# State products of a token mixer moved between two halves of a projection, and convolution pieces at a group's boundary moved ahead of them

## The chip, the cores and the metric

The kernel runs on one core of one Trainium2 chip. The metric is the device time of one execution in microseconds (us). The median of three runs before the change is 2328.43 us (2327.97 to 2331.13). The execution that was profiled took 2326.24 us; its trace spans 2324.4 us from the first to the last instruction.

## The reference

One decoder layer over 2048 tokens of width 1024: a hybrid mixer, cross attention over 256 memory tokens, a mixture of experts, a final norm. The change touches the mixer alone, which projects the normed tokens and runs retention and a Mamba-2 state space (SSD) in chunks of 128 tokens:

```python
proj = hn @ w_in
q, k, v, g, z, xbc, dt_raw, u = jnp.split(proj, splits, axis=-1)
# retention, per chunk
s = einsum('bhcid,bhcjd->bhcij', qc, kc) * decay;  y_in = einsum(s, vc)
kv = einsum('bhcjd,bhcje->bhcde', k_dec, vc)          # carried state S of retention
# SSD, per chunk, after a causal convolution of 4 taps and silu on xbc
CB = einsum('bclgn,bcsgn->bcgls', Cc, Bc)
y_diag = einsum(CB * Lmat, xdt)
states = einsum('bclgn,bclgrp->bcgrpn', Bc, xdt * decay_states)
S = S * chunk_decay + states                           # carried state S of the SSD
y_off = einsum('bclgn,bcgrpn->bclgrp', Cc, S_prev) * exp(A_cum)
```

## The kernel before, in words

The mixer handles 16 chunks q of 128 tokens in 4 groups g of 4 chunks. The order of the work on every engine is written out by hand: each engine has its own list of steps, and the engines meet through semaphores that count finished instructions.

At a group's start TensorE (PE) turns the group's normed rows into eight tiles of columns (turn, L849). ScalarE (ACT) writes the near half-precision part of each (take_hn, L502), and VectorE (DVE) writes the rest that is left over (hn_rest, L622). Every projection is then three half-precision products for each of eight tiles, 24 matmuls of 128x512 in a row (products, L111). First the eight pieces of the convolution's input are projected for the whole group (project_conv); the first of them waits until all eight rests are there. ACT copies each out of PSUM (L512), DVE convolves it (L632 to L643).

Then the chunks follow one another. While PE works on chunk q it also projects chunk q+1, in pieces put between the small products of chunk q: dt and u (project_dt), queries and keys (project_qk), value and gate columns (project_vg, two halves of 12 matmuls each), z (project_z). The small products of a chunk, in this order, are:

- turn_qk_x (L910, L914), decays (L922, L924), segments (L931);
- inner: C times B (L937) and queries times keys (L942);
- states: C times the carried SSD state (L949), and B times the decayed inputs (L955). L955 writes the PSUM bank that holds C times B, so it waits until DVE's first mask (L718) has read that bank;
- retained: retention's outputs (L118 with vb and S_r) and its new state (L970);
- results: the SSD's inner outputs (L118 with xdt and E).

The small products share three PSUM banks in turn (room); the projections have four other banks (slot) and one for queries and keys. DVE's list for a chunk is: segment inputs (L703), steps of dt (L672 to L698), xdt (L707), decayed xdt (L712), rotation of the next chunk's queries and keys (rotate, L660 to L666), the masks (weights: L718, L721, L724), in the first chunk of a group also the norm of the next group's rows (L603, L606), states (L730, L733, L736), retained (L743 to L747), results (L752 to L765).

The last chunk of a group is handled at the boundary, among the turns and convolution pieces of the next group, and there are three such boundaries; the 16th chunk is handled alone at the end. In the 12 other chunks the loop over q runs. The lists are in the functions marked vector and tensor; L775 to L787 and L991 to L1000 are the boundaries, L1017 to L1030 PE's loop over chunks.

Of the kernel before, what the change touches and what calls it, by code (L numbers as in the profile page):

```python
# [27 lines left out]
KT = D // P  # L28
# [200 lines left out]
def mixer_projections(nc, env, dram, rooms, begun):  # L229
# [5 lines left out]
    with ExitStack() as ctx:  # L235
# [364 lines left out]
        def _(dve):  # L600
# [19 lines left out]
            def hn_rest(g, kt):  # L620
                dve.wait_ge(taken, g * BIG + kt + 1)
                dve.scalar_tensor_tensor(hn_s[1][:, kt, :], bank[kt % 4][:, :], gmix_s[:, kt:kt + 1], hn_s[0][:, kt, :], ALU.mult, ALU.subtract).then_inc(hn_lo, 1)  # L622
# [77 lines left out]
            def segments(q):  # L700
                dve.wait_ge(dt_ready, q + 1)
                dve.wait_ge(ch_done, q)
                dve.tensor_tensor(segin[:, :, :], bc(le, 1, SH), bc(dtA[:, q % GC, :], 2, P), ALU.mult).then_inc(seg_ready, 1)  # L703

            def steps_in(q):
                dve.wait_ge(s_act, q * N_ACT + 2)
                ch.post(dve.tensor_tensor(xdt[:, :, :], xtok[:, :, :], bc(dt_[:, q % GC, :], 2, SP_), ALU.mult))  # L707
                ch.wait()
# [58 lines left out]
            for g in range(NG):  # L767
                q0 = g * GC
                if g:
                    q = q0 - 1  # L770
                    segments(q)
                    hn_rest(g, 0)
                    hn_rest(g, 1)
                    steps_in(q)
                    hn_rest(g, 2)  # L775
                    hn_rest(g, 3)
                    steps_decayed(q)
                    hn_rest(g, 4)
                    hn_rest(g, 5)
                    weights(q)  # L780
                    hn_rest(g, 6)
                    hn_rest(g, 7)
                    states(q)
                    conv(g, 0)
                    retained(q)
                    conv(g, 1)
                    results(q)  # L787
                else:
                    for kt in range(KT):
                        hn_rest(g, kt)  # L790
                    for i in range(1, N_E):
                        early_rest(i)
                    dve.wait_ge(a_set, 1)
                    dve.wait_ge(k_ld, 32)
                    dve.wait_ge(c_ld, 16 * 11)
                    dve.tensor_scalar(a_bc[:, :], a_bc[:, :], -1.0, None, ALU.mult).then_inc(a_set, 1)
                    dve.wait_ge(a_set, 2)
                    dve.wait_ge(w_lo, N_E)
                    dve.wait_ge(s_set, 5)
                    conv(g, 0)  # L800
                    conv(g, 1)
                for ct in range(2, KT):
                    conv(g, ct)
                dt_bias(q0)
                dt_one(q0)
                dt_rest(q0)
                rotate(q0)
                for q in range(q0, q0 + GC - 1):
                    segments(q)
                    dt_bias(q + 1)  # L810
                    steps_in(q)
                    dt_one(q + 1)
                    steps_decayed(q)
                    dt_rest(q + 1)
                    rotate(q + 1)
                    weights(q)
                    if q == q0 and g < NG - 1:
                        norm(g + 1)
                    states(q)
                    retained(q)  # L820
                    results(q)
            q = NCH - 1
# [12 lines left out]
        def _(pe):  # L835
# [8 lines left out]
            def turn(g, kt):  # L844
                o = slot(g, kt)
                if kt == 0:
                    pe.wait_ge(xs_done, g * GC + GC)
                for c in range(GC):
                    ins = pe.transpose(o[:, c * P:(c + 1) * P], xg[:, c, kt * P:(kt + 1) * P], ident)  # L849
                ins.then_inc(big, 1)  # L850

            def project_conv(g, ct):
                if g == 0 and ct % 2 == 0:
                    pe.wait_ge(w_lo, ct // 2 + 1)
                if ct == 0:
                    pe.wait_ge(taken, g * BIG + KT)
                    pe.wait_ge(hn_lo, g * KT + KT)
                o = slot(g, KT + ct)
                w = [[wi[:, h, kt, C_XBC + ct * P:C_XBC + (ct + 1) * P] for kt in range(KT)] for h in range(2)]
                hn = [[hn_s[h][:, kt, :] for kt in range(KT)] for h in range(2)]  # L860
                products(pe, o[:, :], w, hn).then_inc(big, 1)
# [19 lines left out]
            def project_vg(q, half):  # L881
                g, n = q // GC, 2 * KT + 3 * (q % GC) + 1
                ins = project(q, bank[n % 4] if half else slot(g, n), C_VG, 2 * RW, HALF[half])
                if half:
                    ins.then_inc(big, 1)
# [47 lines left out]
            def inner(q):  # L933
                tok = slice(q % GC * P, (q % GC + 1) * P)
                o = room(q, 5)
                for k in range(2):
                    ins = pe.matmul(o[:, k * P:(k + 1) * P], xc[:, 4 + k, tok], xc[:, 6 + k, tok], start=True, stop=True)  # L937
                ins.then_inc(small, 1)
                pe.wait_ge(s_act, q * N_ACT + 1)
                o = room(q, 6)  # L940
                for h in range(RH):
                    ins = pe.matmul(o[:, h * P:(h + 1) * P], kT[:, h // 2, :], qz[:, h // 2, h % 2, :], start=True, stop=True)  # L942
                ins.then_inc(small, 1)

            def states(q):
                tok = slice(q % GC * P, (q % GC + 1) * P)
                o = room(q, 7)
                for k in range(2):
                    ins = pe.matmul(o[:, k * 256:(k + 1) * 256], xc[:, 6 + k, tok],  # L949
                                    S_m[:, 4 * k:4 * k + 4, :].rearrange("p h e -> p (h e)"), start=True, stop=True)  # L950
                ins.then_inc(small, 1)
                o = room(q, 8)
                pe.wait_ge(s_dve, q * N_DVE + 1)
                for k in range(2):
                    ins = pe.matmul(o[:, k * 256:(k + 1) * 256], btok[:, k, :], xdec[:, k * 256:(k + 1) * 256], start=True, stop=True)  # L955
                ins.then_inc(small, 1)
# [23 lines left out]
            for g in range(NG):  # L980
                q0 = g * GC
                if g:
                    q = q0 - 1
                    turn_qk_x(q)
                    turn(g, 0)
                    turn(g, 1)
                    decays(q)
                    turn(g, 2)
                    turn(g, 3)
                    segments(q)  # L990
                    turn(g, 4)  # L991
                    turn(g, 5)
                    inner(q)
                    turn(g, 6)
                    turn(g, 7)
                    states(q)
                    project_conv(g, 0)
                    retained(q)
                    project_conv(g, 1)
                    results(q)  # L1000
                else:
                    for kt in range(KT):
                        turn(g, kt)
                    project_conv(g, 0)
                    project_conv(g, 1)
                for ct in range(2, KT):
                    project_conv(g, ct)
                if g == 0:
                    pe.wait_ge(w_lo, N_E)
                project_dt(q0)  # L1010
                if g == 0:
                    pe.wait_ge(l_lo, KT)
                for part in (project_qk, project_vg, project_z):
                    part(q0, 0)
                    part(q0, 1)
                for q in range(q0, q0 + GC - 1):
                    turn_qk_x(q)  # L1017
                    project_dt(q + 1)
                    decays(q)
                    segments(q)  # L1020
                    project_qk(q + 1, 0)
                    project_qk(q + 1, 1)
                    inner(q)
                    states(q)
                    project_vg(q + 1, 0)
                    project_vg(q + 1, 1)
                    retained(q)
                    results(q)
                    project_z(q + 1, 0)
                    project_z(q + 1, 1)  # L1030
            q = NCH - 1
# [1849 lines left out]
```

## Time and profile before

| | before |
|---|---|
| median of three runs | 2328.43 us (2327.97 to 2331.13) |
| profiled execution | 2326.24 us |
| its span | 2324.4 us, 43924 instructions |
| PE busy | 2121.5 us (91%) |
| DVE busy | 1449.3 us (62%) |
| ACT busy | 974.8 us (42%) |
| POOL busy | 502.6 us (22%) |
| mean granted TensorE clock | 0.966 |

The mixer is the first 679 us of the span; the S5 mixer, the attention and the experts follow, each behind a barrier of all engines. A row of the timeline gives the start in us from the span's start, how long the row lasted, the engine, line and operation, what it wrote and read, how many instructions it merges, and in brackets how long the engine had been idle before it and who ended that. Consecutive matmuls overlap in the pipeline, so the time that a block holds PE is read from the start of one row to the start of the next, not from a row's length. A float32 matmul stands in the trace as two records.

### The profile page before, as it was taken

The page shows a single profiled execution, that of the slowest core. Times are in us where ns is not written, and L with a number is a line of the kernel's source. Part 1 is how long each engine was busy: PE and PEld are TensorE (multiplying, and loading weights), DVE is VectorE, ACT ScalarE, POOL GpSimd, SP SyncE. Part 2 cuts the span into 40 slices and gives each one's busy share as a digit, 9 for nine tenths or more (in the row PEclk, how much of TensorE's full clock was granted, in tenths as well). Part 3 has the DMA queues.
Part 4 walks back from the last instruction along what each step waited for, and adds up shares of the span by engine and source line. Part 5 has one row for each costly group of instructions (what it writes and reads, how often), then busy time and mean ns, then how long its engine had stood idle before and what let it go on. Part 6 is the DMA issues. An engine that isn't in the chain of part 4 may idle for free. (4 is left out here: it accounts for less than half of the span.)

```text
span 2324.4 us, 43924 instructions
## 1 busy us (share of the span) xinstructions
PE 2121.5 (91%) x15061; PEld 1207.6 (52%) x15062; DVE 1449.3 (62%) x2501; ACT 974.8 (42%) x1470; POOL 502.6 (22%) x378
## 2 busy tenths in 40 slices
PE   7999999999979897999999999659999999999990
PEld 3455554555658873455555555325555555555450
DVE  7566565665668864344445454477566777777763
ACT  5432533333321333222222222147566677667653
POOL 0022121121220000001111011133333443444433
PEclk9999999999989999999999999879999999999995
DMA  8101001011050134112112110089889999999958
GB/s 254 51 28 64 1 28 64 1 28 48 10 227 28 56 127 173 55 37 73 46 64 73 37 46 37 37 305 353 256 277 315 325 342 347 344 336 332 343 167 305
DMA packets 160842, 350.96 MB, mean 151 GB/s; under 512 B 29866, under 2 KB 40490, under 8 KB 160464
## 3 DMA queue, kind: packets, MB, share of 16 engines
q1 hardware_dynamic: 140416, 311.37, 36.8%
q0 software_dynamic: 19152, 33.74, 6.4%
q10 hardware_dynamic: 1152, 4.19, 0.5%
q8 instruction: 80, 1.31, 0.2%
q14 instruction: 42, 0.34, 0.0%
HBM read 299.94 MB, written 58.26 MB: 154 GB/s over the span
## 5 line engine op out<-in xcount | busy, mean ns | idle before, releaser
L2690 PE MATMUL bankE<-wgu,xT 128*64 128x512 f16 x3840 | 429.9, 380 | 20.1 <-issue 11.7
L2690 PEld LDWEIGHTS bankE<-wgu,xT 128*64 128x64 f16 x3840 | 218.3, 110 | 223.1 <-issue 36.7
L2587 DVE SCALAR_TENSOR_TENSOR wgu<-w_rows,wgu 128x2048 f16<-128x2048 f32 x128 | 284.8, 2286 | 37.2 <-ACT wgu L2441 37.1
L111 PE MATMUL bankA<-main_room,hnT 128*128 128x512 f16 (+1 forms) x1536 | 303.2, 355 | 4.1 <-DVE main_room L646 4.1
L2389 POOL DMA_INDIRECT scratch_ybuf<-y,rows x80 | 173.2, 2165 | 376.6 <-DMA scratch_ybuf<-y,rows 276.5
L2441 ACT ACTIVATE wgu<-w_rows 128x2048 f16<-128x2048 f32 x128 | 234.3, 1899 | 34.4 <-issue 27.0
L111 PEld LDWEIGHTS bankA<-main_room,hnT 128*128 128x128 f16 x1536 | 149.9, 98 | 148.5 <-issue 10.3
L2690 PE MATMUL bankE<-wd,hT 128*64 128x512 f16 x1920 | 222.5, 381 | 0.4 <-ACT hT L2472 0.4
L2587 DVE SCALAR_TENSOR_TENSOR wd<-w_rows,wd 128x2048 f16<-128x2048 f32 x64 | 143.8, 2288 | 54.5 <-ACT wd L2441 51.7
L111 PE MATMUL bankA<-hnT,main_room 128*128 128x512 f16 x768 | 169.0, 381 | 8.9 <-issue 6.8
L111 PE MATMUL bankC<-w_out_s,catT 128*128 128x512 f16 x768 | 170.1, 382 | 2.5 <-DVE w_probs L2056 2.5
L111 PE MATMUL vbank<-w_probs,probsT 128*128 128x512 f16 x768 | 171.9, 381 | 0.0
L111 PE MATMUL bankC<-main_room,hnT_c 128*128 128x512 f16 x768 | 170.7, 379 | 0.0
L2690 PEld LDWEIGHTS bankE<-wd,hT 128*64 128x64 f16 x1920 | 102.1, 110 | 96.1 <-issue 13.9
L1887 POOL TENSOR_TENSOR rs_c<-ms_c,nhalf_c 128x1 f32<-128x1 f32 x32 | 17.7, 554 | 557.1 <-DVE ms_c L2016 557.1
L2381 POOL DMA_INDIRECT xr<-scratch_xn_scr,rows x82 | 119.5, 1457 | 78.5 <-PE bankE L2663 46.4
L2441 ACT ACTIVATE wd<-w_rows 128x2048 f16<-128x2048 f32 x64 | 118.9, 1903 | 26.6 <-issue 25.3
L111 PEld LDWEIGHTS bankA<-hnT,main_room 128*128 128x128 f16 x768 | 74.8, 98 | 100.0 <-issue 12.4
L111 PEld LDWEIGHTS bankC<-w_out_s,catT 128*128 128x128 f16 x768 | 75.4, 98 | 91.7 <-DVE w_probs L2056 3.4
L111 PEld LDWEIGHTS bankC<-main_room,hnT_c 128*128 128x128 f16 x768 | 75.2, 98 | 84.1
L111 PEld LDWEIGHTS vbank<-w_probs,probsT 128*128 128x128 f16 x768 | 74.2, 98 | 85.1 <-issue 1.3
L2599 DVE SCALAR_TENSOR_TENSOR sg<-bankE,gate_of,sg 128x256 f32<-128x256 f32 x80 | 38.3, 479 | 92.7 <-ACT sg L2462 92.5
(390 smaller groups left out, 2992.1 us busy)
## 6 DMA issues: line engine op xcount, KB each, us to landing
w_rows<-in_w_gate SPq DMA_DIRECT2D x64, 1024.0 KB, 8.3
w_rows<-in_w_up SPq DMA_DIRECT2D x64, 1024.0 KB, 9.6
w_rows<-in_w_down SPq DMA_DIRECT2D x64, 1024.0 KB, 9.1
cat_t<-scratch_cat SPq DMA_DIRECT2D x16, 512.0 KB, 4.8
main_room<-in_x SPq DMA_DIRECT2D x16, 512.0 KB, 5.6
scratch_ybuf<-main_room SPq DMA_DIRECT2D x16, 512.0 KB, 2.6
out<-hf SPq DMA_DIRECT2D x16, 512.0 KB, 11.1
x_room<-in_x SPq DMA_DIRECT2D x3, 2048.0 KB, 10.9
```

Of the source, the lines that this page charges most:

```text
L111: ins = pe.matmul(o, a[x][k], b[y][k], start=start and k == 0 and j == 0, stop=stop and k == n - 1 and j == 2)
L1887: pool.tensor_tensor(rs[:, k, c:c + 1], ms[:, k, c:c + 1], nhalf[:, 0:1], ALU.pow).then_inc(rsd, 1)
L2381: pool.indirect_dma_start(xr[:, b % 2, :], None, from_rows, bass.IndirectOffsetOnAxis(ap=rows[:, b:b + 1], axis=0), bounds_check=2 * T - 1 ...
L2389: pool.indirect_dma_start(to_rows, bass.IndirectOffsetOnAxis(ap=rows[:, b:b + 1], axis=0), y[b % 2], None, bounds_check=2 * T - 1, oob_is_ ...
L2441: act.activation(place(p, slot, 0), room(p), ACT.Copy, scale=W_SCALE).then_inc(done, 1)
L2587: dve.scalar_tensor_tensor(place(p, slot, 1), room(p), W_SCALE, place(p, slot, 0), ALU.mult, ALU.subtract).then_inc(done, 1)
L2599: dve.scalar_tensor_tensor(sg[:, p, :], GB[p][:, DE // 2:], gate_of[:, bass.ds(b, 1)], sg[:, p, :], ALU.mult, ALU.mult).then_inc(hr, 1)
L2690: ins = pe.matmul(o(half), tokens(x, k), rows(z, k, half), start=k == 0 and j == 0, stop=k == n - 1 and j == 2, skip_group_check=True)
```

## The change

On PE, in the 12 chunks of the loop, the first half of the next chunk's value and gate columns goes ahead of the state products, which then stand between the two halves. At the three boundaries the first convolution piece goes ahead of the state products, and the second ahead of retention's products. On DVE, at the boundaries, the three masks go behind all eight rests (before, two rests stood behind them). Nothing is added or removed. ACT, POOL and the DMA queue on SP keep their order.

```diff
@@ vector, boundary
                     steps_decayed(q)
-                    hn_rest(g, 4)
-                    hn_rest(g, 5)
+                    for kt in range(4, KT):
+                        hn_rest(g, kt)
                     weights(q)
-                    hn_rest(g, 6)
-                    hn_rest(g, 7)
                     states(q)
                     conv(g, 0)
@@ tensor, boundary
                     turn(g, 7)
+                    project_conv(g, 0)
                     states(q)
-                    project_conv(g, 0)
+                    project_conv(g, 1)
                     retained(q)
-                    project_conv(g, 1)
                     results(q)
@@ tensor, loop over chunks
                     inner(q)
+                    project_vg(q + 1, 0)
                     states(q)
-                    project_vg(q + 1, 0)
                     project_vg(q + 1, 1)
                     retained(q)
                     results(q)
```

PE in the loop over chunks, before: state products (L949, L955) right behind the inner products (L937, L942), then the 24 matmuls of the next chunk's value and gate columns (L111), then retention (L118).

```order
L937 MATMUL bankA<-xc 128x128
L942 MATMUL bankA<-qz,PT 128x128 [waits small_taken_act]
L942 MATMUL bankA<-qz,PT 128x128 x3
L949 MATMUL bankA<-S_m,xc 128x256 [waits small_taken_act]
L949 MATMUL bankA<-S_m,xc 128x256
L955 MATMUL bankA<-segin,btok 128x256 [waits small_taken_dve]
L955 MATMUL bankA<-segin,btok 128x256
L111 MATMUL bankA<-main_room,hnT 128x512 [waits big_taken]
L111 MATMUL bankA<-main_room,hnT 128x512 x23
L118 MATMUL bankA<-vb,PT 64x64 [waits small_taken_dve,big_taken]
```

Here L955 is the first instruction behind the inner products that waits for DVE. The same place now; the file is two lines shorter above it, so L935, L940, L947 and L953 are the former L937, L942, L949 and L955.

```order
L935 MATMUL bankA<-xc 128x128
L940 MATMUL bankA<-qz,PT 128x128 [waits small_taken_act]
L940 MATMUL bankA<-qz,PT 128x128 x3
L111 MATMUL bankA<-main_room,hnT 128x512 [waits big_taken]
L111 MATMUL bankA<-main_room,hnT 128x512 x11
L947 MATMUL bankA<-S_m,xc 128x256 [waits small_taken_act]
L947 MATMUL bankA<-S_m,xc 128x256
L953 MATMUL bankA<-segin,btok 128x256 [waits small_taken_dve]
L953 MATMUL bankA<-segin,btok 128x256
L111 MATMUL bankA<-main_room,hnT 128x512 x12
L118 MATMUL bankA<-vb,PT 64x64 [waits small_taken_dve,big_taken]
```

Twelve of the 24 matmuls have moved ahead of the state products; the instruction that waits for DVE's mask (semaphore small_taken_dve) now stands behind them.

PE at a boundary now, from the last turns (L847, formerly L849): the first convolution piece, with its wait for the rests (hn_rest), stands right behind the turns.

```order
L847 MATMUL bankA<-cst_a,x_room 128x128 [waits hn_rest,big_taken]
L847 MATMUL bankA<-cst_a,x_room 128x128 x3
L111 MATMUL bankA<-hnT,main_room 128x512 [waits big_taken,hn_rest]
L111 MATMUL bankA<-hnT,main_room 128x512 x23
L947 MATMUL bankA<-S_m,xc 128x256 [waits small_taken_act]
L947 MATMUL bankA<-S_m,xc 128x256
L953 MATMUL bankA<-segin,btok 128x256 [waits small_taken_dve]
L953 MATMUL bankA<-segin,btok 128x256
L111 MATMUL bankA<-hnT,main_room 128x512 [waits hn_rest,big_taken]
L111 MATMUL bankA<-hnT,main_room 128x512 x23
L118 MATMUL bankA<-vb,PT 64x64 [waits small_taken_dve,big_taken]
```

Before, the two state products stood between the turns and that piece, and the second piece stood behind retention's products.

DVE at a boundary, before: rests (L622) on both sides of the masks (L718, L721, L724).

```order
L712 TENSOR_TENSOR segin<-xdt,dec 128x512 [waits small_taken_act]
L622 SCALAR_TENSOR_TENSOR hnT<-bankA,gmix_s,hnT 128x512 [waits big_taken,dve_steps_a]
L622 SCALAR_TENSOR_TENSOR hnT<-bankA,gmix_s,hnT 128x512 [waits big_taken]
L718 TENSOR_TENSOR PT<-bankA,cst_a 128x256 [waits small_done]
L721 TENSOR_TENSOR E<-E,PT 128x1024 [waits small_taken_dve]
L724 TENSOR_TENSOR PT<-bankA,cst_a 128x512 [waits small_done,dve_steps_a]
L622 SCALAR_TENSOR_TENSOR hnT<-bankA,gmix_s,hnT 128x512 [waits big_taken,small_taken_dve]
L622 SCALAR_TENSOR_TENSOR hnT<-bankA,gmix_s,hnT 128x512 [waits big_taken]
L730 TENSOR_TENSOR segin<-bankA,dec 128x512 [waits small_done]
```

The last two rests, for which the first convolution piece waits, stand behind the masks here. DVE at a boundary now:

```order
L712 TENSOR_TENSOR segin<-xdt,dec 128x512 [waits small_taken_act]
L622 SCALAR_TENSOR_TENSOR hnT<-bankA,gmix_s,hnT 128x512 [waits big_taken,dve_steps_a]
L622 SCALAR_TENSOR_TENSOR hnT<-bankA,gmix_s,hnT 128x512 [waits big_taken] x3
L718 TENSOR_TENSOR PT<-bankA,cst_a 128x256 [waits small_done]
L721 TENSOR_TENSOR E<-E,PT 128x1024 [waits small_taken_dve]
L724 TENSOR_TENSOR PT<-bankA,cst_a 128x512 [waits small_done,dve_steps_a]
L730 TENSOR_TENSOR segin<-bankA,dec 128x512 [waits small_done,small_taken_dve]
```

The masks have moved behind the last two rests, straight ahead of the state step (L730).

## Rows read from the trace of the kernel before

**Rows 1.** Page, busy time, share of the span and instructions of each engine.
```profile
PE 2121.5 (91%) x15061; PEld 1207.6 (52%) x15062; DVE 1449.3 (62%) x2501; ACT 974.8 (42%) x1470; POOL 502.6 (22%) x378
```

**Rows 2.** Waits, 0 to 560 us: total us, times, longest us.
```profile
PEld bankA L955 <- DVE PT L718: 9.5, 12, 0.9
...
PE bankA L111 <- issue: 6.8, 3, 2.3
...
PE bankA L118 <- DVE S_m L736: 0.9, 3, 0.3
```

**Rows 3.** Timeline of PE in one chunk of the loop (columns as told above).
```profile
124.67 5.34 PE L111 MATMUL bankA<-main_room,hnT 128*128 128x512 f16 x24
129.85 0.61 PE L937 MATMUL bankA<-xc 128*128 128x128 f32 x4
130.29 1.06 PE L942 MATMUL bankA<-qz,PT 128*128 128x128 f32 x8
131.19 1.03 PE L949 MATMUL bankA<-S_m,xc 128*128 128x256 f32 x4
132.73 1.10 PE L955 MATMUL bankA<-segin,btok 128*128 128x256 f32 x4 [0.52 <-DVE PT L718]
133.67 5.34 PE L111 MATMUL bankA<-main_room,hnT 128*128 128x512 f16 x24
138.95 0.34 PE L118 MATMUL bankA<-vb,PT 128*64 128x64 f32 x4
...
141.20 5.35 PE L111 MATMUL bankA<-main_room,hnT 128*128 128x512 f16 x24
```

**Rows 4.** Timeline of DVE in the same chunk.
```profile
132.16 0.42 DVE L718 TENSOR_TENSOR PT<-bankA,cst_a 128x256 f32<-128x256 f32 x1
...
134.60 0.69 DVE L730 TENSOR_TENSOR segin<-bankA,dec 128x512 f32<-128x512 f32 x1
...
135.93 0.69 DVE L736 TENSOR_TENSOR S_m<-S_m,bankA 128x512 f32<-128x512 f32 x1
```

**Rows 5.** Timeline of PE in the first chunk of a group.
```profile
112.21 1.15 PE L118 MATMUL bankA<-xdt,E 128*64 128x64 f32 x32 [0.29 <-DVE S_m L736]
```

**Rows 6.** Timeline of DVE in that chunk.
```profile
107.50 2.74 DVE L606 TENSOR_SCALAR x_room<-x_room,rstd_a 128x1024 f32<-128x1024 f32 x4 [1.13 <-POOL rstd_a L414]
...
111.47 0.69 DVE L736 TENSOR_TENSOR S_m<-S_m,bankA 128x512 f32<-128x512 f32 x1
```

**Rows 7.** Timeline of PE at the first boundary, from the last turns.
```profile
182.31 1.04 PE L849 MATMUL bankA<-cst_a,x_room 128*128 128x128 f32 x8
183.19 1.03 PE L949 MATMUL bankA<-S_m,xc 128*128 128x256 f32 x4
184.34 1.10 PE L955 MATMUL bankA<-segin,btok 128*128 128x256 f32 x4
187.72 5.34 PE L111 MATMUL bankA<-hnT,main_room 128*128 128x512 f16 x24 [2.28 <-issue]
...
200.68 14.63 PE L111 MATMUL bankA<-hnT,main_room 128*128 128x512 f16 x67
```

**Rows 8.** Timeline of DVE at that boundary.
```profile
182.45 1.41 DVE L622 SCALAR_TENSOR_TENSOR hnT<-bankA,gmix_s,hnT 128x512 f16<-128x512 f32 x2
183.78 0.41 DVE L718 TENSOR_TENSOR PT<-bankA,cst_a 128x256 f32<-128x256 f32 x1
...
186.21 1.41 DVE L622 SCALAR_TENSOR_TENSOR hnT<-bankA,gmix_s,hnT 128x512 f16<-128x512 f32 x2
...
193.88 0.55 DVE L635 TENSOR_SCALAR xc<-xbcT,cw,cb 128x512 f32<-128x512 f32 x1 [4.27 <-ACT xbcT L512]
```

**Rows 9.** Timeline of ACT at that boundary.
```profile
181.54 2.68 ACT L502 ACTIVATE hnT<-bankA,gmix_s 128x512 f16<-128x512 f32 x4
```

**Rows 10.** Timeline of PE at the third boundary.
```profile
507.62 6.86 PE L111 MATMUL bankA<-hnT,main_room 128*128 128x512 f16 x24 [2.28 <-issue]
```

**Rows 11.** Stretch behind it: length, busy of PE, PEld, DVE, ACT, POOL, granted clock.
```profile
508.00:510.00 2.00, 2.00 (x6) 0.73 (x5) 1.48 (x4) 0.00 (x0) 0.00 (x0) 0.50 0.04 8
```

## The prediction

> **What bounds the kernel now.** I read the busy times first: PE is busy for 91% of the span and every other engine for 62% or less [rows 1], so in the mixer I look for what PE waits for. The waits view of the first 560 us names three kinds at the places that the change touches [rows 2]. The weight load of L955 waits 12 times for DVE's first mask (L718), 9.5 us in all, 0.79 us each. A projection (L111) waits 3 times, 6.8 us in all; the view names no releaser ("issue"). And results (L118) wait 3 times for the carried SSD state (L736), 0.9 us in all. The timelines place them. In a chunk of the loop PE issues L949 at 131.19 us and L955 at 132.73, 0.15 us behind the end of the mask at 132.16 + 0.42 = 132.58 [rows 3, 4]. At a boundary the first convolution piece starts at 187.72, idle for 2.28 us before, 0.10 us behind the end of the last rests (186.21 + 1.41 = 187.62): the unnamed releaser is DVE's L622 [rows 7, 8]. PE has no slack in the loop, since each block starts where the last one ends, so what PE saves there the time saves; the later stages start behind a barrier and are moved as a whole.
>
> **The chunks of the loop.** Nothing is added or removed; twelve matmuls go ahead of four. From L949 to retention the old order takes 138.95 - 131.19 = 7.76 us [rows 3]. The new one, from the same rows: a block of 24 ahead of a float32 product takes 129.85 - 124.67 = 5.18, so the first half 2.59; L955 takes 133.67 - 132.73 = 0.94, and L949, which has the same shape, I put at 0.94 too (it was never seen without the wait behind it); the second half, with the step over to retention, 5.28 - 2.59 = 2.69. The sum is 7.16, which saves 0.60. The split adds two steps between half precision and float32 that no row shows between these very blocks. From below they cost nothing: 5.18 / 24 = 0.216 us a matmul leaves no room for one ahead of L937. From above 0.10 each, the excess of 5.28 over 5.18 ahead of retention. So 0.40 to 0.60 a chunk; I take 0.55, near the row of L937, which is the same kind of step.
>
> Does the wait go? L955 would issue at 131.19 + 2.59 + 0.94 = 134.72, and the mask was read out by 132.58: 2.1 us of cover [rows 3, 4]. What is late next? DVE's state step now follows L949 and L955: it starts at about 134.8 instead of 134.60, and its last part (L736, 0.69 us) waits for the end of L955 near 135.8, so it is over near 137.0 instead of 136.62. Retention starts on PE at 131.19 + 7.16 = 138.35 and results, which need that state, behind it. At least 1.3 us are left. Behind the waiting L730 on DVE stand only the state step and retention's copies, which themselves wait for PE.
>
> In the first chunk of groups 0 to 2 this fails. There DVE puts the norm of the next group's rows (2.74 us, from 107.50) ahead of the state step, which ends at 111.47 + 0.69 = 112.16; results start at 112.21, having waited 0.29 us already [rows 5, 6]. DVE's times there do not depend on the state products, so results still start at 112.21 and what PE saved becomes a longer wait. These 3 chunks give 0 (from below also 0: no instruction of DVE is later). The other 9 of the 12 give 9 x 0.55 = 5.0 us (3.6 to 5.4).
>
> **The three boundaries.** The masks took DVE from 183.78 to 186.21, 2.43 us. Behind all rests now, they let the seventh and eighth rest start at 183.78, if ACT has written those tiles: its four copies end at 181.54 + 2.68 = 184.22, 0.67 each, so the seventh is there at 183.55 and the eighth before 184.45, when DVE comes to it [rows 8, 9]. The rests end at 185.19, and the first convolution piece starts at 185.29, 2.43 us earlier. But the state products stood in that idle time for nothing, and now they are on PE's path with 2 x 0.94 = 1.88 us. Block by block: 185.29 + 5.18 (piece) + 1.88 + 5.28 (second piece up to retention) + 2.25 (retention and results, 141.20 - 138.95 in rows 3) = 199.88 for the third piece, which started at 200.68 [rows 3, 7]. That saves 0.80 a boundary. The lower end leaves the four blocks from 187.72 to 200.68 as long as they were together (12.96): 2.43 - 1.88 = 0.55. The upper end is 0.90, one step of 0.10 less. I take 0.80, since the rows of the loop show the very sequence retention, results, projection: 2.4 us for the three (1.7 to 2.7).
>
> The change adds a wait on DVE: L730 now stands until L949 is over at 185.29 + 5.18 + 0.94 = 191.4, while the masks are done at about 187.5. Queued behind it are the rest of the state step and the convolution of the first piece. The state step ends near 193.4, and L635, which waited for ACT until 193.88 [rows 8], starts at about 193.7. So the convolution is not later, and PE does not wait for it: the pieces use four banks that ACT empties.
>
> **The sum.** 5.0 + 2.4 = 7.4 us. On the profiled execution this is 2326.2 - 7.4 = 2318.8. That execution was 2.2 us under the median of the runs; against the median the forecast is 2328.4 - 7.4 = 2321.0 us.
>
> **The clock, weighed.** At the third boundary the same block that lasts 5.34 elsewhere lasted 6.86 us, behind the same 2.28 us of idleness; in the stretch from 508 to 510 the granted clock was 0.50, the lower level of 1.2 GHz, with PE busy all through [rows 7, 10, 11]. It cost 1.52 us in one of three boundaries. The pause stays, shorter: from the end of the turns at 182.31 + 1.04 = 183.35 to 185.29, 1.9 us, with nothing in it. The forecast leaves this cost as it is. The Trainium skill (TensorE: Matmul & The Clock Gate, "HAM oscillation — how this bites in real kernels") says that a kernel whose matmul bursts stand behind waits can lose the clock at every such wait and begin every burst cold. [...]
>
> **Rivals.** (B) The wait only moves: in every chunk of the loop results wait for the carried state, as they do in the first chunk. For it: the state products end about 2 us later relative to DVE's list, and rows 5 show this wait. Against it: at least 1.3 us are left without the norm. Then the loop gives nothing and the boundaries 2.4: 2326.0, no change. (C) The clock falls at all three boundaries, for as long as it did at one: 2 x 1.52 = 3.0 us lost, 2324.0. For it: PE's work ahead of the pause is now turns alone; against it: the pause is shorter and no boundary but one paid. (D) Slower: the same fall lasts through the whole first piece at all three boundaries, since that piece now follows the turns directly. Each of 24 matmuls then takes 0.216 us more, 5.18 a boundary, 15.5 in all, of which 1.5 are paid already: 2321.0 + 14.0 = 2335.0. It decides from 8.9 us lost at the boundaries (7.4 gained and 1.5 paid), about 14 slow matmuls at each. Against it: the one fall seen cost 1.52, seven matmuls. That the order on PE isn't what the code says is excluded, since it is written out by hand.
>
> **How the numbers follow.** The forecast has 0.73, B 0.08, C 0.14, D 0.05. About 0.2% (4.7 us) is what a measurement of this kernel can tell from no change. Of the forecast's 0.73 I count 0.06 as within that bound (its lower end is 5.3 us), of C 0.03 as faster. So faster 0.67 + 0.03 = 0.70; within 0.06 + 0.08 + 0.11 = 0.25; slower 0.05. The forecast's own range is 2328.4 less 8.1 to 5.3: 2320.3 to 2323.1. The low end, 2317.0, adds the clock not falling at all (1.5) and the scatter of a median; the high end, 2327.5, takes in B and C with the same scatter. D stays outside.
>
> **What would show it.** Right: L953 (formerly L955) has no wait left in the loop; from the end of the inner products to retention PE needs about 7.2 us; results wait about 0.8 us in three chunks and nowhere else; the first piece starts about 1.9 us behind the turns, and the third comes 0.8 us earlier after them than before. Wrong: more than 7.4 us from the inner products to retention (the steps between the formats are dear), results waiting in all chunks (B), a granted clock of 0.50 behind every boundary (C, D), or a stage behind the mixer that takes back what came early.

## The result and the profile after

The changed kernel takes 2314.76 us in the median of four runs (2309.87 to 2315.63), beside 2329.24 us for the kernel before in four runs; the ratio is 0.9944, 95% interval 0.9924 to 0.9963. Timed again beside 17 runs of before it was 0.9956 (0.9941 to 0.9972). So by the two ratios it is faster by about 10 to 13 us, where 7.4 were forecast, and the first median lies 2.2 us under the lower end of the forecast range (2317.0).

| | before | after |
|---|---|---|
| profiled execution | 2326.24 us | 2315.63 us |
| its span | 2324.4 us | 2313.7 us |
| S5 mixer's first matmul on PE | 679.09 us | 667.85 us |
| mean granted TensorE clock | 0.966 | 0.967 |

The mixer ends 11.24 us earlier and the whole span is 10.7 us shorter: the gain is the mixer's, and the later stages only follow (from S5's first matmul to the end of the span they took 1645.3 us before and 1645.9 after). The first thing to look for is the chunk of the loop that [rows 3] show, now in the changed kernel; the timeline of PE, with the columns of before:

```profile
131.25 2.75 PE L111 MATMUL bankA<-main_room,hnT 128*128 128x512 f16 x12
133.84 1.03 PE L947 MATMUL bankA<-S_m,xc 128*128 128x256 f32 x4
134.70 1.03 PE L953 MATMUL bankA<-segin,btok 128*128 128x256 f32 x4
135.56 2.75 PE L111 MATMUL bankA<-main_room,hnT 128*128 128x512 f16 x12
138.25 0.34 PE L118 MATMUL bankA<-vb,PT 128*64 128x64 f32 x4
...
140.50 5.35 PE L111 MATMUL bankA<-main_room,hnT 128*128 128x512 f16 x24
...
180.85 1.04 PE L847 MATMUL bankA<-cst_a,x_room 128*128 128x128 f32 x8
183.81 5.34 PE L111 MATMUL bankA<-hnT,main_room 128*128 128x512 f16 x24 [1.93 <-DVE hnT L622]
188.99 1.03 PE L947 MATMUL bankA<-S_m,xc 128*128 128x256 f32 x4
189.85 1.03 PE L953 MATMUL bankA<-segin,btok 128*128 128x256 f32 x4
190.72 5.34 PE L111 MATMUL bankA<-hnT,main_room 128*128 128x512 f16 x24
...
198.24 17.01 PE L111 MATMUL bankA<-hnT,main_room 128*128 128x512 f16 x78
```

From the inner products to retention PE now needs 138.25 - 131.25 = 7.00 us, not 7.76: the saving is 0.76 a chunk. L953 has no wait, and both state products take 0.86 (134.70 - 133.84, 135.56 - 134.70), where the trace of before showed 0.94 for L955. The lower rows are the first boundary, the counterpart of [rows 7]: from the last turns to the third piece 198.24 - 180.85 = 17.39 us, not 18.37.

The waits of PE and of its weight loads (PEld) from 0 to 560 us in the changed kernel:

```profile
PE bankA L111 <- DVE hnT L622: 7.9, 4, 2.1
...
PEld bankA L118 <- DVE S_m L736: 3.0, 3, 1.0
PE bankA L118 <- DVE S_m L736: 2.6, 3, 0.9
```

Of the 7.9 us, 2.1 belong to the start of the program; three are the pauses at the boundaries, 1.93 each. The three waits of results for the carried state are the first chunks of groups 0 to 2; they grew from 0.29 to 0.87 us, as the row that answers [rows 5] shows. DVE's step that they wait for (the second row) has stayed where it was: it ends at 112.22, where [rows 6] had 112.16, and the chunks began 0.06 us later.

```profile
112.28 1.15 PE L118 MATMUL bankA<-xdt,E 128*64 128x64 f32 x32 [0.87 <-DVE S_m L736]
...
111.53 0.69 DVE L736 TENSOR_TENSOR S_m<-S_m,bankA 128x512 f32<-128x512 f32 x1
```

At the third boundary, where [rows 10] had the slow block, the same block in the changed kernel:

```profile
498.71 5.34 PE L111 MATMUL bankA<-hnT,main_room 128*128 128x512 f16 x24 [1.93 <-DVE hnT L622]
```

It lasts 5.34 us instead of 6.86; the granted clock did not fall (1.00 in every stretch of 2 us from 494 to 502). The books close: 9 x 0.76 + 3 x 0.98 + 1.52 = 11.30, and the mixer began its chunks 0.06 us later, which leaves the 11.24.

### The profile page after: what moved, and what is told of

It reads as the page before. It is cut to its first block and busy times, and to the rows that moved or that the text cites. A ratio compares the mean times of both kernels' runs of the same rounds, so it can differ in the third digit from the quotient of the medians.

```text
span 2313.7 us, 43924 instructions
## 1 busy us (share of the span) xinstructions
PE 2115.2 (91%) x15061; PEld 1208.3 (52%) x15062; DVE 1450.6 (63%) x2501; ACT 974.2 (42%) x1470; POOL 498.0 (22%) x378
## 5 line engine op out<-in xcount | busy, mean ns | idle before, releaser
L2688 PE MATMUL bankE<-wgu,xT 128*64 128x512 f16 x3840 | 430.4, 380 | 19.9 <-issue 13.4
L111 PE MATMUL bankA<-main_room,hnT 128*128 128x512 f16 (+1 forms) x1536 | 305.3, 355 | 4.1 <-DVE main_room L646 4.1
L111 PEld LDWEIGHTS bankA<-main_room,hnT 128*128 128x128 f16 x1536 | 149.9, 98 | 145.9 <-issue 10.4
L111 PE MATMUL bankA<-hnT,main_room 128*128 128x512 f16 x768 | 167.4, 379 | 7.9 <-DVE hnT L622 7.9
L111 PE MATMUL bankC<-w_out_s,catT 128*128 128x512 f16 x768 | 171.0, 383 | 2.5 <-DVE w_probs L2054 2.5
L111 PE MATMUL vbank<-w_probs,probsT 128*128 128x512 f16 x768 | 173.1, 383 | 0.0
L111 PE MATMUL bankC<-main_room,hnT_c 128*128 128x512 f16 x768 | 170.7, 379 | 0.0
L111 PEld LDWEIGHTS bankA<-hnT,main_room 128*128 128x128 f16 x768 | 74.6, 98 | 97.6 <-issue 8.7
L111 PEld LDWEIGHTS bankC<-w_out_s,catT 128*128 128x128 f16 x768 | 75.8, 99 | 92.4 <-DVE w_probs L2054 3.4
L111 PEld LDWEIGHTS vbank<-w_probs,probsT 128*128 128x128 f16 x768 | 74.5, 99 | 86.0 <-issue 2.8
L111 PEld LDWEIGHTS bankC<-main_room,hnT_c 128*128 128x128 f16 x768 | 75.2, 98 | 84.1
## 6 DMA issues: line engine op xcount, KB each, us to landing
out<-hf SPq DMA_DIRECT2D x16, 512.0 KB, 11.4
```

The costliest lines, as they stand in the source:

```text
L111: ins = pe.matmul(o, a[x][k], b[y][k], start=start and k == 0 and j == 0, stop=stop and k == n - 1 and j == 2)
L2688: ins = pe.matmul(o(half), tokens(x, k), rows(z, k, half), start=k == 0 and j == 0, stop=k == n - 1 and j == 2, skip_group_check=True)
```

## The experiments

**One part at a time.** The theory of the waits says that the gains of loop and boundaries add up on PE. The rival says that what exceeds the forecast comes from the clock at the boundaries. Four kernels, ten runs each, beside 31 runs of before (median 2327.57 us).

The loop alone:

```diff
@@ tensor, loop over chunks
                     inner(q)
+                    project_vg(q + 1, 0)
                     states(q)
-                    project_vg(q + 1, 0)
                     project_vg(q + 1, 1)
```

> Only PE's loop over chunks is changed; the boundaries stay as before. The theory of the waits: nine chunks lose the wait of L955 for DVE's mask, 0.76 us each as in the changed kernel's trace, the three first chunks of a group nothing: 6.8 us less than before, period of a chunk 27.14 instead of 27.90 us, and the S5 mixer's first matmul at about 672.2 instead of 679.1 us (1.5 earlier or not by the clock at a boundary). The rival theory of the clock (what the change gave beyond its forecast comes from boundaries at which the clock no longer falls): also 6.8 here, and the rest of the gain has to show in the run on the boundaries alone.

Measured: 2323.01 us, ratio 0.9982 (0.9970 to 0.9995). S5 begins at 672.15 us, 6.94 earlier; the period of a chunk is 27.14 us. PE's timeline at the second boundary, which is as before in this kernel, and at the start of S5:

```profile
344.38 7.03 PE L111 MATMUL bankA<-hnT,main_room 128*128 128x512 f16 x24 [2.29 <-issue]
...
672.15 0.36 PE L1538 MATMUL bankB<-x_room 16*128 16x16 f32 x2 [11.84 <-PEq L235]
```

The mixer behaves as the theory of the waits has it. The clock fell at one boundary here too, but at the second. The ratio, 4.2 us with an interval of 1.2 to 7.0, holds the 6.8, but its middle is 2.6 us short of it: single executions of before range from 2320.32 to 2331.99, and what they follow is shown under "The clock of every execution" below.

The boundaries alone, both engines (the two boundary parts of the change):

> Only the boundaries are changed, on PE and on DVE; the loop stays as before. The theory of the waits: three boundaries of 25.41 instead of 26.39 us from the chunk's first turn to the third convolution piece, 2.9 us less than before, and at most 1.5 more where before the clock fell at one. The rival theory of the clock: before, it falls in most executions at two or three boundaries, and here at none, so that up to 4.5 us come on top: 6 to 7.5 us less.

Measured: 2321.59 us, ratio 0.9975 (0.9964 to 0.9986), S5 at 674.62 us, 4.47 earlier. PE's timeline:

```profile
182.29 1.04 PE L847 MATMUL bankA<-cst_a,x_room 128*128 128x128 f32 x8
185.26 5.34 PE L111 MATMUL bankA<-hnT,main_room 128*128 128x512 f16 x24 [1.93 <-DVE hnT L622]
...
199.69 4.49 PE L111 MATMUL bankA<-hnT,main_room 128*128 128x512 f16 x20
```

17.40 us from the last turns to the third piece, so 0.97 a boundary, 2.9 in all, and 1.5 of the clock, which fell at no boundary. Loop and boundaries add up: 6.94 + 4.47 = 11.41, beside 11.24 for both. (The clock fell at the third boundary in the trace of before, at the second in the loop's, and at none in the other two.) Both theories have a share: of the 4.47 us in the trace, 2.9 are waits and 1.5 the clock, and the median's 6.0 us are more than the 2.9 of the waits.

The boundaries on PE alone (DVE keeps the masks ahead of the last two rests):

> Only PE's order at the boundaries is changed; on DVE the masks still stand ahead of the last two rests. The theory of the waits: the first piece starts 5.4 us behind the last turns as before, and the state products, which stood in that pause, are on the path: 5.41 + 14.43 = 19.84 instead of 18.37 us from the last turns to the third piece, 1.5 a boundary, 4.4 us slower than before, and more if the longer idle stretch makes the clock fall. If PE's order is what gains, faster by up to 2.9.

Measured: 2333.58 us, ratio 1.0031 (1.0019 to 1.0042). Slower, and by more than the 4.4 us of the order: S5 begins 9.5 us later. PE's timeline at the three boundaries:

```profile
181.19 1.04 PE L849 MATMUL bankA<-cst_a,x_room 128*128 128x128 f32 x8
186.60 8.08 PE L111 MATMUL bankA<-hnT,main_room 128*128 128x512 f16 x24 [4.37 <-DVE hnT L622]
...
203.77 0.60 PE L111 MATMUL bankA<-hnT,main_room 128*128 128x512 f16 x2
...
350.75 7.92 PE L111 MATMUL bankA<-hnT,main_room 128*128 128x512 f16 x24 [4.38 <-DVE hnT L622]
...
514.74 7.85 PE L111 MATMUL bankA<-hnT,main_room 128*128 128x512 f16 x24 [4.37 <-DVE hnT L622]
```

The pause is 4.37 us, and behind it the first piece runs at the lower clock at all three boundaries (8.08, 7.92 and 7.85 us instead of 5.34). The granted clock at the third, in the columns of [rows 11]:

```profile
513.00:515.00 2.00, 0.26 (x1) 0.14 (x2) 1.60 (x3) 0.00 (x0) 0.00 (x0) 0.51 0.00 0
515.00:517.00 2.00, 2.00 (x6) 0.73 (x5) 0.00 (x0) 0.00 (x0) 0.00 (x0) 0.50 0.04 8
517.00:519.00 2.00, 2.00 (x7) 0.63 (x5) 0.00 (x0) 0.00 (x0) 0.00 (x0) 0.50 0.00 0
519.00:521.00 2.00, 2.00 (x9) 0.85 (x8) 0.00 (x0) 0.00 (x0) 0.00 (x0) 0.79 0.00 0
```

The clock is down before the piece begins and for some 5 us of it (to about 519.8, by the 0.79 of the last stretch). This is what rival C of the prediction feared, a fall at every boundary, brought about by a longer pause; it costs 2.5 to 2.7 us each time, more than C's 1.52 and less than D's 5.18.

The boundaries on DVE alone (all rests ahead of the masks; PE as before):

> Only DVE's order at the boundaries is changed: all eight rests, then the masks; PE is as before. The theory of the waits: L955 now waits for the first mask, which ends about 185.5 on the clock of rows 7 and 8, so it starts at 185.7 and the first piece at 186.6 instead of 187.7: 1.1 us a boundary, 3.3 us less than before, as much as both parts of the boundary together. If DVE's order needs PE's to gain, no change (within 1 us).

Measured: 2322.26 us, ratio 0.9975 (0.9962 to 0.9987), the same as with both. PE's timeline:

```profile
182.00 1.04 PE L847 MATMUL bankA<-cst_a,x_room 128*128 128x128 f32 x8
182.87 1.03 PE L947 MATMUL bankA<-S_m,xc 128*128 128x256 f32 x4
185.34 1.10 PE L953 MATMUL bankA<-segin,btok 128*128 128x256 f32 x4 [1.43 <-DVE PT L718]
186.27 5.34 PE L111 MATMUL bankA<-hnT,main_room 128*128 128x512 f16 x24
...
199.23 5.14 PE L111 MATMUL bankA<-hnT,main_room 128*128 128x512 f16 x23
```

17.23 us from the last turns to the third piece, 1.14 a boundary, as expected from the rows. That is 0.16 more than the change gives with PE's part. At the boundaries DVE's order is the whole gain from the waits, and PE's order on top of it gives back a little. The clock fell at none of these three boundaries either: with PE's order of before, the longest pause is now the 1.43 us ahead of L953.

**The wait removed in another way.** If the loop's gain is the wait, it must also come with PE untouched and the mask earlier on DVE:

```diff
@@ vector, loop over chunks
-                    rotate(q + 1)
-                    weights(q)
+                    if q == q0 and g < NG - 1:
+                        rotate(q + 1)
+                        weights(q)
+                    else:
+                        weights(q)
+                        rotate(q + 1)
```

> PE keeps the order of before everywhere. On DVE, in nine chunks of the loop (not in the first chunk of groups 0 to 2), the three masks go ahead of the rotation, so the first mask is read out some 1.7 us before L955 issues. The theory of the waits: what the split gained was the wait and nothing else, so the same 0.76 us a chunk come from DVE's side: chunks of 27.14 instead of 27.90 us, 6.8 us less than before, the S5 mixer's first matmul near 672.2 us or 1.6 more or less by the clock at a boundary. The rival theory of the order (two halves of a projection around float32 products pipeline better by themselves): no more than the idle time that PE's row shows, 0.52 us a chunk, 4.7 us in all. On the clock: the boundaries are those of before, idle for 2.28 us; it should fall at one of three, as in the two traces so far.

Measured: 2321.96 us, ratio 0.9984 (0.9973 to 0.9995) beside 17 runs of before. PE's timeline of a chunk (L953 and L959 are the former L949 and L955), and below it the first pieces at the three boundaries:

```profile
131.15 1.03 PE L953 MATMUL bankA<-S_m,xc 128*128 128x256 f32 x4
132.01 1.03 PE L959 MATMUL bankA<-segin,btok 128*128 128x256 f32 x4
132.88 5.34 PE L111 MATMUL bankA<-main_room,hnT 128*128 128x512 f16 x24
...
140.40 5.35 PE L111 MATMUL bankA<-main_room,hnT 128*128 128x512 f16 x24
...
186.15 7.02 PE L111 MATMUL bankA<-hnT,main_room 128*128 128x512 f16 x24 [2.28 <-issue]
...
346.27 7.03 PE L111 MATMUL bankA<-hnT,main_room 128*128 128x512 f16 x24 [2.29 <-issue]
...
506.39 7.03 PE L111 MATMUL bankA<-hnT,main_room 128*128 128x512 f16 x24 [2.28 <-issue]
```

From the first state product to the z projection 140.40 - 131.15 = 9.25 us; after the change, from the first half to the same block, 140.50 - 131.25 = 9.25; before, 141.20 - 131.19 = 10.01. The same 0.76 to the hundredth, with no split: the wait was the whole gain, and splitting the block costs nothing. The rival of the order falls. The clock did not do as expected: it fell at all three boundaries, 1.68 us each, so S5 begins only 3.4 us earlier (675.73). The measured ratio (1.2 to 6.3 us by its interval) does not hold the expected 6.8 either.

**Where the first chunks lose.** The norm behind the state step, on the changed kernel:

```diff
@@ vector, loop over chunks
+                    states(q)
                     if q == q0 and g < NG - 1:
                         norm(g + 1)
-                    states(q)
                     retained(q)
```

> The changed kernel, with the norm of the next group's rows moved behind the state step on DVE in the first chunk of groups 0 to 2. If those chunks gave nothing because of the norm, results no longer wait there for L736 (0.87 us each in the changed kernel): 3 x 0.87 = 2.6 us less than the changed kernel, S5's first matmul near 665.2 instead of 667.85 us. If DVE as a whole is what bounds those chunks, the wait moves to the next chunk's segment inputs and nothing is gained.

Measured in a single run: 2310.61 us; S5 begins at 663.76 us. PE's timeline of the first chunk, from one chunk's first turn to the next one's:

```profile
89.91 0.60 PE L908 MATMUL bankA<-cst_a,qr 128*128 128x128 f32 x4
...
110.83 1.10 PE L118 MATMUL bankA<-xdt,E 128*64 128x64 f32 x32
...
117.05 0.60 PE L908 MATMUL bankA<-cst_a,qr 128*128 128x128 f32 x4
```

The same two turns in the changed kernel, and in the kernel before:

```profile
90.13 0.60 PE L908 MATMUL bankA<-cst_a,qr 128*128 128x128 f32 x4
...
118.55 0.60 PE L908 MATMUL bankA<-cst_a,qr 128*128 128x128 f32 x4
```

```profile
90.07 0.60 PE L910 MATMUL bankA<-cst_a,qr 128*128 128x128 f32 x4
...
118.49 0.60 PE L910 MATMUL bankA<-cst_a,qr 128*128 128x128 f32 x4
```

The chunk takes 27.14 us, like the others, and 28.42 in the changed kernel (118.55 - 90.13). So the norm's place was the reason, and the wait marked 0.87 was worth 1.28: 3.8 us in the three chunks, not the expected 2.6.

**The change again, and a faster version.**

> The changed kernel as it is, timed again beside many runs of before. The mixer ends 11.24 us earlier in the profiles, 1.52 of it by a fall of the clock in one trace of before; with such a fall at a third of the boundaries of before and at none of the change the mean is 9.8 + 1.6 = 11.3 us, a ratio of 0.9952. The rival: the first four runs, 14.5 us under before in the median, show a further gain in the stages behind the mixer: 0.994 or less.

Measured: 2315.37 us in six runs (2310.65 to 2319.32), ratio 0.9956 (0.9941 to 0.9972). The ratio stands nearer to the 0.9952 of the first theory; 0.994 lies just outside the interval. The clock fell at none of its three boundaries. In this execution the chunks begin at 88.10 us and S5 at 665.89, both about 2 us earlier than in the first trace of the same kernel (90.13 and 667.85): when the start of S5 is compared between single traces, the start of the chunks has to be taken off.

The last one has the norm as above and, at the boundaries, the state products in PE's pause, with the first mask between the sixth and the seventh rest (weights is split into first_mask and other_masks, with the same instructions):

```diff
@@ vector, boundary
-                    for kt in range(4, KT):
-                        hn_rest(g, kt)
-                    weights(q)
+                    hn_rest(g, 4)
+                    hn_rest(g, 5)
+                    first_mask(q)
+                    hn_rest(g, 6)
+                    hn_rest(g, 7)
+                    other_masks(q)
                     states(q)
@@ tensor, boundary
+                    states(q)
                     project_conv(g, 0)
-                    states(q)
                     project_conv(g, 1)
```

> The changed kernel with the norm behind the state step, and at the boundaries the state products back in PE's pause: on DVE the first mask stands between the sixth and the seventh rest, so L955 can start 0.15 us behind it; then the two convolution pieces, retention, results. On the clock of rows 7 and 8: mask until 184.2, L955 at 184.3, rests until 185.65, first piece at 185.75, third at 185.75 + 5.18 + 5.28 + 2.25 = 198.5 instead of 199.7 by the change. The theory of the waits: 3 x 1.2 + 2.6 = 6.2 us less than the changed kernel, S5's first matmul near 661.6 us, about 17 us under before. If the boundaries are bounded by the rests whatever stands in the pause, 2.6 less only.

Measured: 2305.98 us in six runs (2304.32 to 2308.17), ratio 0.9915 (0.9902 to 0.9928), 9.4 us under the change in the same comparison. S5 begins at 658.71 us. PE's timeline (L956 and L962 are the state products):

```profile
178.46 1.04 PE L856 MATMUL bankA<-cst_a,x_room 128*128 128x128 f32 x8
179.33 1.03 PE L956 MATMUL bankA<-S_m,xc 128*128 128x256 f32 x4
180.48 1.10 PE L962 MATMUL bankA<-segin,btok 128*128 128x256 f32 x4
181.75 10.52 PE L111 MATMUL bankA<-hnT,main_room 128*128 128x512 f16 x48 [0.17 <-issue]
...
194.45 2.76 PE L111 MATMUL bankA<-hnT,main_room 128*128 128x512 f16 x12
```

The pause has gone: 15.99 us from the last turns to the third piece, 1.40 less than the change. With the norm this is 3 x 1.40 + 3 x 1.28 = 8.0 us, where 6.2 were expected; S5 begins 9.14 earlier, of which 1.12 are an earlier start of the chunks (89.01 instead of 90.13).

**The clock of every execution.** Each timed execution has its mean granted clock on record, to a thousandth, and the time goes with it: of the 31 runs of before, the eight at 0.964 took 2330.22 us in the mean and the six at 0.967 took 2324.39, about 1.9 us for each thousandth. With this slope the gains can be put at one clock. The fourth column is such an estimate; the last is what the traces give to the waits alone.

| kernel | mean clock (before) | mean gain, us | gain at the same clock, estimate | waits in the trace |
|---|---|---|---|---|
| loop alone | 0.9648 (0.9655) | 5.2 | 6.6 | 6.8 |
| boundaries, both engines | 0.9672 (0.9655) | 5.8 | 2.6 | 2.9 |
| boundaries on PE alone | 0.9641 (0.9655) | -6.6 | -3.9 | -4.4 |
| boundaries on DVE alone | 0.9667 (0.9655) | 5.7 | 3.5 | 3.4 |
| masks first | 0.9651 (0.9662) | 4.1 | 6.3 | 6.8 |
| the change again | 0.9673 (0.9662) | 11.4 | 9.4 | 9.8 |
| norm and state products too | 0.9668 (0.9662) | 19.9 | 18.8 | 17.8 |

Once the clock is taken out, every kernel gains what its waits say, within about 1 us, and the change shows no further gain behind the mixer. The rest goes with the clock: some 2 to 3 us for the change and the two kernels with DVE's new order at the boundaries, 1 for the last kernel. The two kernels that make the loop faster and leave the boundaries as they were ran at a lower mean clock than before, which by this estimate is why their medians show only some 4 us. Why their clock is lower is not shown, and the numbers do not say where in the span it was lost.

## Why the prediction was wrong

**Right.** What bounds the mixer, where the waits stand, that L955's wait goes and nothing takes its place in nine chunks, that the three first chunks give nothing (28.42 us against 118.49 - 90.07 = 28.42 before), that the first piece starts 2.43 us earlier after the turns (2.45), that the convolution on DVE is not later, and that the later stages only follow.

**Mis-sized: the chunks, 5.0 forecast, 6.84 measured.** The step that failed is "L955 takes 133.67 - 132.73 = 0.94, and L949, which has the same shape, I put at 0.94 too". That 0.94 was read behind a wait; without it the products take 0.86 each. Of the 0.21 a chunk, 0.16 is this, and 0.05 is the price that I put on the two steps between the formats, which cost nothing. The rows of before had a nearer price: L937, four records of half as many columns, held PE for 130.29 - 129.85 = 0.44 us, twice which is 0.88. The masks-first run shows 0.76 as the price of the wait by itself: before, L955 started 1.54 us behind L949 instead of 0.86, and the next block 0.94 behind L955 instead of 0.86, which is 0.68 + 0.08.

The idle times in the views are not this price. The 0.79 us a wait that the prediction read from [rows 2] is a mean of two kinds, nine waits in the loop and three at the boundaries. The weight loads of the trace before, in the chunk of [rows 3] and at the boundary of [rows 7]:

```profile
132.70 0.73 PEld L955 LDWEIGHTS bankA<-segin,btok 128*128 128x128 f32 x4 [0.89 <-DVE PT L718]
...
184.31 0.73 PEld L955 LDWEIGHTS bankA<-segin,btok 128*128 128x128 f32 x4 [0.49 <-DVE PT L718]
```

So in the loop the weight load's row marks 0.89 and PE's row 0.52, one too much and one too little; that the mean of 0.79 is near 0.76 is luck. PE's bracket is short mainly because it counts from the end of a row: L949's row lasts 1.03 us, while the next product can start 0.86 behind it.

**Mis-sized by the same step: the boundaries, 2.4 forecast, 2.94 measured.** The state products on the path took 1.73 instead of 1.88 us, which is 0.15 of the 0.18 a boundary. With these two terms alone the forecast would have been 2328.4 - 9.8 = 2318.6, still inside the range.

**Failed: "The forecast leaves this cost as it is."** I saw that the pause gets shorter, 2.28 to 1.93 us, and priced only a worse clock (C, D). The better case stood in the low end of the range alone. In the traces the clock fell behind 5 of 9 pauses of 2.28 us (before, loop alone, masks first), at 1.5 to 1.7 us each, behind none of 12 of 1.93 us, and behind 3 of 3 of 4.37 us. At that rate, an estimate from three traces, the old boundaries lose about 2.7 us in the mean (3 x 5/9 x 1.6); the mean clocks of the runs give 2 to 3. The change gives them back: 6.84 + 2.94 + 2.7 = 12.5, which the intervals of both ratios hold. This term, put at nothing, is the one that takes the result out of the range (2328.4 - 12.5 = 2315.9); what is left to the measured 2314.76 is within the scatter of the base.

**The base.** The forecast counts from 2328.4 us, the median of three runs. Later groups of before had medians of 2327.57 and 2325.95, and the first four runs of the change were 0.6 us under its later median. Such scatter is as large as what remains, and it is not a step of the argument.

**Rivals.** B is refuted: in the loop results wait for the state in the three first chunks only (and, for 0.6 us as before, in the 16th, which is handled alone). C and D did not occur. If PE's order is changed without DVE's, the clock falls at all three boundaries as in C, for longer than C had it.

## What to carry to other kernels

Price a wait by the period of the loop without it, or from the start of one row to the start of the next against the same product in steady flow, not by the idle time that a view marks: in the loop PE's row marked 0.52 and the weight load's 0.89 where the wait was worth 0.76, and in the first chunks 0.87 and 1.0 where it was 1.28. Work that stood in a pause for nothing costs its full time once it is moved out: before reordering the engine that waits, move what the other engine does first, and keep work in the pause. A shorter pause on TensorE can pay twice, since the clock may stop falling behind it. Put timed runs at the same granted clock before comparing small gains.

## What the runs showed of the hardware

Two float32 products of 128x256 behind one another took 0.86 us each in steady flow, and the block behind a product that had waited started 0.94 us after it: 0.08 us of the wait's price lie behind the instruction that waits. Putting a half-precision block in two parts around float32 products cost nothing measurable (9.25 us either way). The fall of the clock behind a pause does not come each time that the same code runs: pauses of 2.28 us were followed by it in 1, 1 and 3 of three boundaries in three traces (granted clock 0.50, 1.5 to 1.7 us lost). With the changed order on PE, 1.93 us never brought it (0 of 12) and 4.37 us always did (3 of 3); what lies between was not tried with this order. The scatter between executions of one kernel goes with the granted clock, about 1.9 us for each thousandth of its mean.
